# Stick breaking's gates: from plain weight blocks beside the attention steps to a fourth seven-product multiplication, with a trip through DRAM

## What is computed

```python
def even_layer(x, pre_g, post_g, w_in, conv_w, b_i, b_f, hn_g, w_out):
    h = rmsnorm_2(x, pre_g)
    u = h @ w_in
    qa, ka, va, oa, za, ia, fa, qb, kb, vb, zb = split_cols(u, EVEN_SPLITS)
    ...
    ha = mlstm(qa, ka, va, ig, lf)
    ha = jax.nn.sigmoid(oa) * ha
    ya = head_norm(ha, hn_g, A_HEADS) * jax.nn.silu(za)
    hb = stick_breaking(heads(qb), heads(kb), heads(vb))
    yb = hb * jax.nn.silu(zb)
    y = jnp.concatenate([ya, yb], axis=-1) @ w_out
    return x + rmsnorm_2(y, post_g)
```

## Time and profile before

| | us |
|---|---|
| median of 3 runs | 1903.16 (1903.15 to 1906.49) |
| the profiled execution | 1904.67 |
| its span, first to last instruction | 1902.9 |
| PE busy in the span | 1890.5 (99%) |
| PEld busy | 1586.6 (83%) |
| DVE busy | 920.9 (48%) |
| ACT busy | 871.6 (46%) |
| POOL busy | 1048.0 (55%) |

### The profile page before, as it was taken

The page is one execution under the profiler, slowest core; times in us unless marked ns, Lnnn a source line. Parts: engine busy times, 40 slices in busy tenths (PEclk is TensorE's granted clock), DMA queues, the critical chain, the costliest instruction groups (busy, mean ns, idle before and its releaser), DMA issues.

```text
span 1902.9 us, 25281 instructions
## 1 busy us (share of the span) xinstructions
PE 1890.5 (99%) x9034; PEld 1586.6 (83%) x9034; DVE 920.9 (48%) x1384; ACT 871.6 (46%) x1689; POOL 1048.0 (55%) x1289
## 2 busy tenths in 40 slices
PE   9999999999999999999999999999999999999998
PEld 7878888898888988888889888888788789888887
DVE  3531321431023397778647854877355545024652
ACT  5522443423333454554456543376456746333332
POOL 5732644443465598788845733356444465545572
PEclk9999999999999999999999999999999999999999
DMA  6341433232233432333242321676222242323331
GB/s 233 104 110 45 133 84 90 73 93 67 78 111 100 144 100 89 110 101 122 67 133 73 106 78 45 149 205 144 78 67 73 64 142 79 101 87 90 99 116 51
DMA packets 105293, 191.82 MB, mean 101 GB/s; under 512 B 10940, under 2 KB 16680, under 8 KB 105182
## 3 DMA queue, kind: packets, MB, share of 16 engines
q1 hardware_dynamic: 95956, 173.56, 30.5%
q0 software_dynamic: 3456, 6.29, 2.0%
q10 hardware_dynamic: 5770, 10.49, 1.6%
HBM read 184.27 MB, written 6.02 MB: 100 GB/s over the span
## 4 chain that ended last, share of the span: by engine, by line
PE 95%; DVE 2%; ACT 1%; DMA 0%; issue 0%; SPq 0%; POOL 0%; DVEq 0%; ACTq 0%
PE proj L2509 24%; PE proj L2511 23%; PE proj L2510 23%; PE work L2936 2%; PE work L2937 2%; PE work L2935 2%; PE proj L2658 1%; PE proj L2657 1%; PE proj L2656 1%; PE work L3097 1%; PE work L3077 1%; PE work L2510 1%; PE work L2511 1%; PE work L2509 1%; PE work L2885 1%; PE work L2682 1%
## 5 line engine op out<-in xcount | busy, mean ns | idle before, releaser
L778 POOL TENSOR_TENSOR w_lo<-w_raw,w_hi 128x256 fp32r<-128x256 f32 x1080 | 865.4, 834 | 733.0 <-ACT w_hi L849 732.5
L849 ACT CAST w_hi<-w_raw 128x512 fp32r<-128x512 f32 x564 | 333.4, 619 | 437.8 <-PE proj L2511 359.3
L2509 PE MATMUL proj<-act_hi,w_hi 128*128 128x512 f32 (+1 forms) x1312 | 496.1, 378 | 0.6 <-DVE act_lo L1668 0.3
L2511 PE MATMUL proj<-act_hi,w_lo 128*128 128x512 f32 (+1 forms) x1312 | 490.4, 374 | 0.0
L2510 PE MATMUL proj<-act_lo,w_hi 128*128 128x512 f32 (+1 forms) x1312 | 490.3, 374 | 0.0
L2509 PEld LDWEIGHTS proj<-act_hi,w_hi 128*128 128x128 f32 x1312 | 247.1, 188 | 44.9 <-DVE arena L1880 0.7
L2511 PEld LDWEIGHTS proj<-act_hi,w_lo 128*128 128x128 f32 x1312 | 247.0, 188 | 44.1
L2510 PEld LDWEIGHTS proj<-act_lo,w_hi 128*128 128x128 f32 x1312 | 247.2, 188 | 43.8 <-issue 0.5
L2509 PE MATMUL proj<-w_hi,act_hi 128*128 128x512 f32 x576 | 231.7, 402 | 0.4 <-DVE arena L2370 0.3
L2511 PE MATMUL proj<-w_hi,act_lo 128*128 128x512 f32 x576 | 225.3, 391 | 0.0
L2510 PE MATMUL proj<-w_lo,act_hi 128*128 128x512 f32 x576 | 225.0, 391 | 0.0
(11 more groups left out here) (415 smaller groups left out, 2755.3 us busy)
## 6 DMA issues: line engine op xcount, KB each, us to landing
w_raw<-in_w_in SPq DMA_DIRECT2D x154, 256.0 KB, 2.7
w_raw<-in_w_in_ab SPq DMA_DIRECT2D x134, 256.0 KB, 2.7
w_raw<-in_w_mlp SPq DMA_DIRECT2D x72, 256.0 KB, 2.9
w_raw<-in_w_in_c SPq DMA_DIRECT2D x64, 256.0 KB, 2.7
arena<-in_w_mlp SPq DMA_DIRECT2D x28, 512.0 KB, 4.0
w_raw<-in_w_out_ab SPq DMA_DIRECT2D x32, 256.0 KB, 2.7
w_raw<-in_w_out_c SPq DMA_DIRECT2D x32, 256.0 KB, 2.7
arena<-in_w_in_ab SPq DMA_DIRECT2D x24, 256.0 KB, 4.1
```

The costliest lines, as they stand in the source:

```text
L778: ins = pool.tensor_tensor(w_lo[:, slot, c], raw_of(b)[:, c], w_hi[:, slot, c].bitcast(F32), ALU.subtract)
L849: act.copy(w_hi[:, b % RING, :], raw_of(b)).then_inc(hi_ready, 1)
L2509: pe.matmul(out_, a_hi, b_hi, start=first, stop=False)
L2511: return pe.matmul(out_, a_lo, b_hi, start=False, stop=last)
```

## The change

`sb_z` becomes a fourth Seven, computed second of the four (behind `lstm_o`). Its eight gate pieces go through ACT's Silu into the four slots of `gate_tmp` and from there in four DMAs of 512 KB to DRAM. In step 18 ACT issues two DMAs of 1 MB that bring them back, the first half into the later place of `y`, the second into `sb_gate`. DVE multiplies the outputs of units 0 to 19 by them in five operations, in steps 21, 22, 25, 26 and 29, and from unit 20 on `output` multiplies instead of copying. `gates` and its table loads are gone from the steps. `BESIDE` deals 32 blocks (`sb_q[1]`, `sb_k[1]`, `even_out0[0]`, `even_out0[1]`) to the 35 steps: steps 1, 5, 17, 21, 25, 29 and 33 have none, steps 3, 12, 14 and 34 two, the others one. The buffers `kept` of the Sevens change places, and the load into the first waits for an earlier event.

```diff
-    sevens = [Seven(name, w_ab, at) for name, at in (("lstm_o", 3 * D), ("lstm_z", 4 * D), ("sb_v", at_b + 2 * D))]
+    sevens = [Seven(name, w_ab, at) for name, at in (("lstm_o", 3 * D), ("sb_z", at_b + 3 * D), ("lstm_z", 4 * D),
+                                                          ("sb_v", at_b + 2 * D))]
     for half in range(2):
         for at, name in enumerate(("sb_q", "sb_k")):
             slab(name, w_ab, at_b + at * D + half * NCOL)
             if half == at == 0:
                 slabs.extend(sevens)
-    slab("even_out0", W["w_out_ab_2"], 0)
     for i in range(2):
-        slab("sb_z", w_ab, at_b + 3 * D + i * NCOL)
-    slab("even_out0", W["w_out_ab_2"], NCOL)
+        slab("even_out0", W["w_out_ab_2"], i * NCOL)
...
-        for s, kept_at in zip(sevens, (0, 14336, 0)):
+        for s, kept_at in zip(sevens, (14336, 0, 14336, 0)):
...
+        first_gate = y[:, :, NCOL:D]
...
-        BESIDE = ((2, 1, 1, 2, 2), (1, 1, 2, 1, 1, 2), (2, 1, 1, 1, 1, 2), (1, 1, 2, 1, 1, 2), (2, 2, 1, 1, 1, 1), (1, 1, 2, 1, 1, 2))
+        BESIDE = ((1, 0, 1, 2, 1), (0, 1, 1, 1), (1, 1, 1, 2), (1, 2, 1, 1), (0, 1, 1, 1), (0, 1, 1, 1), (0, 1, 1, 1), (0, 1, 1, 1), (0, 2))
...
-                    sp.wait_ge(proj_full, end("lstm_core"))
+                    sp.wait_ge(lstm_upd_full, 8 * (MT - 1))
...
+            def spill(quarter):
+                at, tokens, i = sevens.index(spilled_), (0, 2, 0, 2)[quarter], (0, 1, 1, 0)[quarter]
+                if quarter == 0:
+                    act.wait_ge(a_out, 2 * at + 2)
+                elif quarter == 1:
+                    act.wait_ge(own_out, 2 * at + 2)
+                else:
+                    act.wait_ge(proj_free, spilled_.bank0 + 2 * (quarter - 2) + 2)
+                slot = 2 * (quarter % 2)
+                act.dma_start(gate_dram[:, tokens:tokens + 2, i * NCOL:(i + 1) * NCOL], gate_tmp[:, slot:slot + 2, :])\
+                   .then_inc(dram_spilled, 16)
...
+                    if s is spilled_ and n == 4:
+                        act.wait_ge(dram_spilled, 32 + 16 * 2)
+                    if s is z_ and n == 0:
+                        act.wait_ge(dram_spilled, 32 + 16 * 4)
...
+            gate(spilled_, 0, ACT.Silu, None)
+            prepared_to(spilled_, T4, 3)
+            spill(0)
+            gate(spilled_, 1, ACT.Silu, None)
+            prepared_to(z_, B11, 3)
+            spill(1)
+            gate(spilled_, 2, ACT.Silu, None)
+            prepared_to(z_, T1, 3)
+            spill(2)
+            gate(spilled_, 3, ACT.Silu, None)
+            prepared_to(z_, T2, 3)
+            spill(3)
+            b_from_a(z_)
+            prepared_to(z_, B21, 3)
+            own_from_c(z_)
+            prepared_to(z_, T3, 3)
...
-            def gates(i):
-
-                s = by_name["sb_z"][i]
+            def gates_back():
+                act.wait_ge(dram_spilled, 32 + 16 * 4)
+                act.wait_ge(sb_z_full, SB_UNITS // 2)
+                act.dma_start(first_gate, gate_dram[:, :, 0:NCOL]).then_inc(dram_returned, 16)
                 act.wait_ge(sb_o_full, SB_UNITS // 2)
-                for m in range(MT):
-                    if i:
-                        act.wait_ge(yb_ready, m + 1)
-                    act.activation(sb_gate[:, m, :], bank(s, m), ACT.Silu, scale=even_r[:, m:m + 1]).then_inc(proj_free, 1)
-                act.preload_act_table_set("natural_log_exp_and_others")
+                act.dma_start(sb_gate, gate_dram[:, :, NCOL:D]).then_inc(dram_returned, 16)
 
             act.preload_act_table_set("natural_log_exp_and_others")
             for i in range(SB_STEPS + 1):
-                gated_ahead = 1 <= i <= SB_UNITS and any(s.name == "sb_z" and j == s.n - 1 for s, j in beside[i - 1])
-                if gated_ahead:
-                    weights(i - 1)
                 if 2 <= i < SB_STEPS:
                     weights_copied(i - 2)
                 if i < SB_UNITS:
                     log_terms(i)
-                if 1 <= i <= SB_UNITS and not gated_ahead:
+                if 1 <= i <= SB_UNITS:
                     weights(i - 1)
+                if i == SB_UNITS // 2 + 2:
+                    gates_back()
...
+            GATED_FROM = 5 * SB_UNITS // 8
+            GATED_AT = (21, 22, 25, 26, 29)
+
             def output(u):
                 h, blk = u // MT, u % MT
+                o_ = sb_o[:, blk, h * HD:(h + 1) * HD]
                 vec.wait_ge(sb_o_full, u + 1)
-                vec.tensor_copy(sb_o[:, blk, h * HD:(h + 1) * HD], work[:, 3, 0:HD]).then_inc(sb_o_copied, 1)
+                if u < GATED_FROM:
+                    ins = vec.tensor_copy(o_, work[:, 3, 0:HD])
+                else:
+                    ins = vec.tensor_tensor(o_, work[:, 3, 0:HD], sb_gate[:, blk, h * HD - NCOL:(h + 1) * HD - NCOL], ALU.mult)
+                ins.then_inc(sb_o_copied, 1)
 
             def gated(i):
-                vec.wait_ge(sb_o_copied, SB_UNITS // 2 * (i + 1))
-                for m in range(MT):
-                    vec.wait_ge(proj_free, by_name["sb_z"][i].bank0 + m + 1)
-                    o_ = sb_o[:, m, i * NCOL:(i + 1) * NCOL]
-                    vec.tensor_tensor(o_, o_, sb_gate[:, m, :], ALU.mult).then_inc(yb_ready, 1)
+                if i == 0:
+                    vec.wait_ge(dram_returned, 16 * 3)
+                if i < MT:
+                    vec.wait_ge(sb_o_copied, SB_UNITS // 2)
+                    o_, gate_ = sb_o[:, i, 0:NCOL], first_gate[:, i, :]
+                else:
+                    vec.wait_ge(sb_o_copied, GATED_FROM)
+                    o_, gate_ = sb_o[:, :, NCOL:NCOL + HD], sb_gate[:, :, 0:HD]
+                vec.tensor_tensor(o_, o_, gate_, ALU.mult).then_inc(yb_ready, 1)
...
-                    pe.wait_ge(yb_ready, MT)
+                    pe.wait_ge(yb_ready, MT + 1)
...
-            pe.wait_ge(yb_ready, 2 * MT)
+            pe.wait_ge(sb_o_copied, SB_UNITS)
```

More of the change, by code:

```diff
@@ L686, in load_seven @@
                     ring_loads(B21)
+                else:
+                    sp.wait_ge(proj_full, end("lstm_core"))
                 for k in range(4):
@@ L988, in embedding_copied @@
                 act.wait_ge(proj_free, s.end)
-                act.dma_start(ple_dram[:, :, part], ple_made[:, :, part]).then_inc(ple_spilled, 16)
+                act.dma_start(ple_dram[:, :, part], ple_made[:, :, part]).then_inc(dram_spilled, 16)
             embedding_copied(0)
@@ L1403, in gate @@
                         src, sem_ = proj[:, 2 * (quarter - 2) + m, :], proj_free
-                    dst = gate_tmp[:, n % 4, :] if done else sb_v[i][:, tokens, :]
+                    dst = sb_v[i][:, tokens, :] if s is v_ else gate_tmp[:, n % 4, :]
                     act.activation(dst, src, func, scale=r_).then_inc(sem_, 1)
@@ L1433, in _ @@
             gate(o_, 1, ACT.Sigmoid, lstm_gated)
-            prepared_to(z_, B11, 3)
+            prepared_to(spilled_, B11, 3)
             gate(o_, 2, ACT.Sigmoid, lstm_gated)
             head_squares(0)
-            prepared_to(z_, T1, 3)
+            prepared_to(spilled_, T1, 3)
             gate(o_, 3, ACT.Sigmoid, lstm_gated)
             head_squares(1)
-            prepared_to(z_, T2, 3)
-            b_from_a(z_)
+            prepared_to(spilled_, T2, 3)
+            b_from_a(spilled_)
             head_squares(2)
-            prepared_to(z_, B21, 3)
-            own_from_c(z_)
-            prepared_to(z_, T3, 3)
+            prepared_to(spilled_, B21, 3)
+            own_from_c(spilled_)
+            prepared_to(spilled_, T3, 3)
             ins = head_squares(3)
@@ L1520, in _ @@
                     log_terms(i)
-                if 1 <= i <= SB_UNITS and not gated_ahead:
+                if 1 <= i <= SB_UNITS:
                     weights(i - 1)
+                if i == SB_UNITS // 2 + 2:
+                    gates_back()
                 for s, j in [x_ for later in beside[i:i + 3] for x_ in later]:
                     prepare(s.first + j + 1)
-                for s, j in beside[i]:
-                    if j == s.n - 1 and s.name == "sb_z":
-                        gates(by_name["sb_z"].index(s))
             ahead(by_name["even_out0"][1])
-            fill_hi("act", ACT_AT["yb"], 2, turn=TURN_AT["yb"], after=end("sb_z"))
-            act.wait_ge(yb_ready, 2 * MT)
+            fill_hi("act", ACT_AT["yb"], 2, turn=TURN_AT["yb"], after=end("sb_k"))
+            act.wait_ge(sb_o_copied, SB_UNITS)
             for r in range(2):
@@ L2309, in _ @@
             own_from_b(o_)
+            rests(g_, B11, 3)
+            gated_quarter(o_, 1)
+            rests(g_, T1, 3)
+            gated_quarter(o_, 2)
+            rests(g_, T2, 3)
+            gated_quarter(o_, 3)
+            rests(g_, B21, 3)
+            rests(g_, T3, 3)
+            c_from_b(g_)
+            head_scales(2)
+            rests(g_, B22, 3)
+            rests(g_, T4, 3)
+            own_from_b(g_)
             rests(z_, B11, 3)
-            gated_quarter(o_, 1)
             rests(z_, T1, 3)
```

(4 more changed lines are left out.)

19 lines of the change are left out of this document (9 added, 10 removed).

## The result

The changed kernel takes 1909.94 us (median of 7 runs, 1908.26 to 1912.95), the kernel before 1903.60 in the same comparison (7 runs, 1903.15 to 1906.49): 1.0035 times as long, 95% interval 1.0023 to 1.0047. The forecast was 1907.8 us, slower.

The account below looks back on a forecast made before the run. The prediction took TensorE's own matmul work to bound the kernel. Its terms, -5.44 + 11.2 + 0.4 - 1.33 - 0.27 = +4.6 us, gave 1907.8 us against the median 1903.16, with a range of 1903.0 to 1912.0.

Parts of the forecast that it names:

- Part 1: Fourth Seven adds 38.08 us, 16 blocks taken out of the steps save 43.52: -5.44 us.
- Part 2: Steps without a block: six wait for ScalarE's `weights`, 1.87 us each, 11.2 us; step 33 waits 0.4 us.
- Part 3: Waits that go: -1.33 us in step 29 without `gates`, -0.27 us behind the steps.
- Part 4: Moved work, including ScalarE's wait for the second spill in the third Seven: cost zero, upper bound 2.1 us.
- The spill holds ScalarE: Rival, third Seven: the wait for the spill costs up to 2.1 us more, 1909.9 us; chance 0.10.
- The chain is shorter: Rival, empty steps: shorter waits, also 0.3 us a step off the chain, 1904.6 us, no change; chance 0.14.
- Waits not paid: Rival, empty steps: they cost nothing, only parts 1 and 3 remain, -7.0 us, 1896.1 us; chance 0.10.
- The clock falls: Rival, steps: blocks behind the six gaps run at half pace, 16.3 us more, 1924.1 us; chance 0.03.

Follow-up runs that it names:

- six empty steps: Kernel before, same 48 blocks, but six steps give their block to other steps; no fourth Seven, no spill: 1914.15 us against 1903.29.
- four empty steps: Changed kernel with another dealing table: step 0 has no block, steps 1, 3 and 5 have one, four waiting steps instead of six: 1909.03 us.
- by banks: Changed kernel with the same 32 blocks dealt in quarters, one bank of three matmuls at a time, only step 33 empty: 1902.81 us.
- GpSimd held back: Changed kernel with GpSimd in the third Seven starting B21's low parts only after VectorE's last low part of T2: 1910.20 us.
- spilled twice: Changed kernel with each of the first two spills issued twice and ScalarE waiting for all four transfers: 1913.73 us.
- the second buffer: Changed kernel with the gates' third and fourth quarter in a buffer of their own, so ScalarE need not wait for the first two spills: 1907.80 us.

## Why the prediction was nearly right

The time was forecast 2.1 us too low, inside the range, and on the right side. Some of that is luck. The same changed kernel was measured three times, 6.3, 9.2 and 6.9 us above the kernel before, and 1912.50 us, the second median, lies above the end of the range. The forecast of +4.6 describes the executions whose spill lands in time: with the wait taken away it was +4.1. How many of a handful of executions are late moves the median. By its own steps:

**Part 1, -5.44 us: right.** Four Sevens of 38.08 us each, and TensorE kept its pitch.

**Part 2, 1.87 us for an empty step: right, 0.11 too high.** The row shows an idle of 1.57, with the rough start 1.76 lost. The hand-over from ScalarE's end to TensorE was 0.06 us (1421.62 to 1421.68), not 0.15; 2.17 us behind the scores' start where 2.26 was said. The kernel before with six empty steps gave +10.9 where 11.2 was the term. Step 33 waits 0.47 instead of 0.34, and for VectorE's output, not ScalarE's copy: the wrong one of two waits was priced, 0.13 us short.

**Part 3, -1.33 and -0.27: right.** No gap in step 29 but that of an empty step; behind the steps 1543.98 - 1537.27 = 6.71 us from the turned tile to `even_out1`. The stretch from the first scores to the turned tile is 138.19 us for a forecast of about 139, and the stage +3.84 for +4.6; of the 0.8 between them six steps at 0.11 make up 0.7.

**Part 4, the spill at zero: wrong, and the only step that failed.** The step that failed is the cost of zero for the new wait, with 2.1 us as its bound. Three sizes in it were off. *Slack*: I let the landing begin with the gates; the second spill is issued 2.0 us earlier than that, 6.52 us before the third Seven's first matmul (1220.11 + 2 x 38.08 - 1289.75) where the gates started 4.52 before it (1296.64 - 1292.12), so the slack at the block I looked at is 8.2 us, not 6.2. *Landing*: 6.70, 8.26 and 8.97 us from issue to ScalarE's go-on in three executions of the same program, where I took a value between 2.6 and 6.5, "nearest to the row of the same size and direction". That row came from a stretch where little else ran; the row from a crowd, 8.3, was the nearer for all but the first. *Price*: at that block it is one for one, as I had it:

| kernel | second issue to go-on | less 8.2 | TensorE stood there | stood at the second place |
|---|---|---|---|---|
| the change, first | 6.70 | none | none | none |
| the change, second | 8.26 | 0.06 | 0.05 | 2.89 |
| four empty steps | 8.73 | 0.5 | 0.53 | 2.82 |
| by banks | 8.76 | 0.6 | 0.56 | 2.33 |
| the change, third | 8.97 | 0.8 | 0.76 | 2.70 |
| GpSimd held back | 9.19 | 1.0 | 0.97 | none |
| spilled twice | 12.08 | 3.9 | 3.87 | none |

(Us; the last row counts from the issue of the second spill to the go-on behind its copy. The 0.05 is from the window of 1296 to 1305 us, where TensorE is busy for 8.95 of 9.00.) What I had not seen is the last column: in the four executions with a go-on 8.3 to 9.0 us after the issue, GpSimd's eight halves met VectorE's last low part of T2, some 10 us later, and that cost 2.3 to 2.9 us, with a lower clock behind it in three of the four. That this stand comes from GpSimd's row is shown by holding GpSimd back; that the wait for the spill is what brings the row there is shown by the second buffer: with it, no low part was long and no run came near 1912. The links between (casts, raw blocks, adds) are read from the traces, not tried one by one. Together 3.5 to 5 us where 2.1 was the upper bound. Without the wait the median is 1907.8, with it 1909.9, 1912.5 and 1911.4 in three comparisons.

Like for like, the forecast was +4.6 us, and +6.3 was measured: the parts on the steps 0.8 too high, the spill 2.5 us too low at this median and up to 5 in a single execution. The two misses pull opposite ways, so the total looks better than part 4 deserves.

**The rivals.** The spill holds ScalarE: this is what happened, on top of the forecast's own losses and at about twice its price; 0.10 was too little for a slack of 6.2 us against a range of landings up to 8.3. The chain is shorter: a tenth of a microsecond a step, not 0.23 or more. Waits not paid: refuted by the rows with 1.57. The clock falls: not in the steps, in this kernel or in the one with six empty steps; it fell where I had not looked, behind the stand of 2.9 us in the third Seven.

**Where the gain of 5.44 us went**: the matmuls are gone, but a block was also the cover of ScalarE's chain, and 32 blocks do not cover 35 steps in whole blocks. In banks they do, but for 0.18 us in step 17.

## What to carry to other kernels

When filler work shrinks, count the places that need cover, not its total: a filler of 2.72 us was needed only for 1.76, and cut in quarters it covered all but 0.18 us. A transfer that an engine must wait for is priced by its landing in the busiest stretch that the trace has for its size, and its slack from its issue; if a free buffer can take the wait away, that is safer than an estimate of the landing. And a late engine can cost more than its lateness: follow what piles up behind it to the next meeting of VectorE and GpSimd.

## What the runs showed of the hardware

**One VectorE operation beside a full GpSimd.** A low part with two SBUF operands takes 0.69 us alone. Beside GpSimd's halves it took at most 1.23 in the kernel before, where the two engines alternate; but it took 6.75, 6.68, 6.23 and 6.61 us in four executions in which GpSimd had eight halves ready in a row, as long as all eight. The Trainium skill, "SBUF — State Buffer", section "Who interferes with whom", says that a VectorE instruction with two SBUF inputs contends with a GpSimd instruction that reads SBUF, that the port pair they share is an exclusive lock, and that issue order decides who blocks. The trace agrees that they contend. It also shows a wait for more than one instruction: VectorE is recorded as started at 1307.49, GpSimd's first half at 1307.82, and VectorE waited for eight. The starts recorded overlap the end of the operation before, so who asked first can't be read from them. It goes the other way too: in the fourth Seven of the changed kernel one half of GpSimd, recorded from 1342.11, took 3.41 us instead of about 0.73, beside four additions that VectorE made without a pause from 1342.42 on, in 2.49 us. That row stands in every execution with a fourth Seven (3.40 to 4.09 us), and TensorE waited for it in none.

**The clock behind a stand.** In the third Seven TensorE was granted 0.66 of full speed in a window of 5 us behind a stand of 2.89 us, 0.71 behind one of 3.87, 0.74 behind one of 2.82, 0.84 and 0.82 in and behind one of 2.33, and 1.00 behind one of 2.70. By the first, an estimate of the loss is 1.7 us, 0.34 x 5, with part of the window at the lower of its two levels, 2.4 and 1.2 GHz. Why the stand of 2.70 us was followed by none is open. Stands of 1.57 us, six in the steps, left it at 1.00.

**Landings vary.** The same DMA of 512 KB from the same place in the program let ScalarE go on after 6.70 to 8.97 us in three executions of one program, at a DMA share of 0.71 to 1.10 in the windows of 5 us from 1285 to 1300. Why it varies was not tried.
